# A two-layer decoder step on one core: the S5 tail, the first products and the sine table re-sequenced over four engines

## The chip, the cores and the metric

The kernel runs on one core of a Trainium2 chip. The metric is the device time of one execution in microseconds. Before the change it is 369.06 us (median of 3 runs, 368.89 to 369.34). Five engines run their own instruction streams in order and meet in semaphores: TensorE (PE in the profile, its weight loads PEld), VectorE (DVE), ScalarE (ACT), GpSimd (POOL) and SyncE (SP, which here only issues DMAs).

## The reference

264 tokens (256 of a prompt, 8 single-token samples) pass through two layers. In each, the normalised input goes through one projection, `w_in`, whose 3088 columns feed four head groups; their gated outputs go through `w_out` and are added to the input:

```
h = rmsnorm(x);  proj = h @ w_in
S5:   complex state recurrence over time, y = gelu(C s + D u),  y *= sigmoid(y @ w_glu)
HGRN: gated scan, log_f from hg_f                      -> head rmsnorm
GLA:  gated scan, gate = logsigmoid(lr @ w_up + b)/16  -> head rmsnorm   (lr: 16 columns of proj)
RET:  retention with rotary                            -> head layernorm
x = x + concat(each * silu(z)) @ w_out
```

The new states of all four groups are outputs too. After the second layer comes a last rmsnorm. S5 needs tables of powers of its complex decay, that is exponentials and sines of the parameters, which the kernel computes itself.

## The kernel before

Everything is kept transposed: 128 channels on the partitions, the 264 tokens along the free axis. `w_in` is cut into 25 chunks of 128 columns (`CHUNKS`); the chunk of the GLA low-rank gate, `C_LR`, has 16 real columns and 112 of zeros. SP streams each chunk in two halves of 256 KB through a ring of 12 slots; `project` (L497, by `product`) multiplies a chunk by the 8 tiles of `h` into one of three PSUM banks, and ACT or DVE must have emptied the bank that was used three steps earlier (`ring_free`) before it is written again. A fp32 matmul stands in the trace as two instructions, so a chunk is 16 of them.

The order on each engine is written out by hand at the end of its block: PE's `for i in range(NCH - 1)` runs the chunks in order and hangs the small stages between them (five `level` stages of the gated scans after chunks 7 to 11, then transposes, block states, rotary, retention scores, S5 response and inputs after chunks 18 and 19). After chunk 23 come `s5_outputs` and `gated_outputs` in two parts each, `ret_outputs`, `sample_outputs(0)`, chunk 24, `sample_outputs(1)`, `ret_means`, `glu_gate`, `head_norms`, then the eight products of `w_out`; two of these are fp32, six use operands split in two parts.

DVE starts with `s5_phases` (L1037), which holds a short exponential of the step sizes (the call of `accurate_exp` at its top) and then the phase tables. Then `scale_x` makes `h`, and in layer 0 `accurate_sines` (L1063) and `s5_coefficients` finish the tables; `s5_c` and `s5_b` build the S5 matrices from them (three operations each and part). `gate` makes the gates of the scans from ACT's `gate_logs`, `level_operands` and `level_scores` serve the five levels. `s5_relay` (L1186) copies the S5 input from token order to block order, 24 copies on 32 partitions each; `s5_scan` runs the recurrence; `s5_gelu`, ACT's tanh and `s5_back` (L1381) make the S5 output, the last again with 20 such copies; `gather_outputs` fetches the other groups' outputs, prompt and samples, and the retention state. Then squares, gates, `center`, `s5_mix` and `head_mix` make the operand of `w_out`.

POOL clears three tiles, then multiplies sample states by their decays and issues the DMAs that split the weights of three `w_out` products; ACT negates these weights at L974 between its last silu and the tanh of the gate. SP copies sample values through DRAM to all partitions (`sample_values`, three kinds of four DMAs, one kind behind each of the first `w_out` chunks).

Of the kernel before, what the change touches and what calls it, by code (L numbers as in the profile page):

```python
# [25 lines left out]
ALU = mybir.AluOpType  # L26
# [25 lines left out]
WSLOTS = 6  # L52
EPS = 1e-6
# [5 lines left out]
(C_LR, C_F0, C_F1, C_Q0, C_Q1, C_GQ, C_GK, C_I0, C_I1, C_GV0, C_GV1,  # L59
 C_RQ, C_RK, C_RV0, C_RV1, C_U0, C_U1) = range(NP)  # L60

CHUNKS = [2048, 768, 896, 512, 640, 1536, 1664, 1024, 1152, 1792, 1920, 2320, 2448, 2576, 2704, 0, 128,
# [66 lines left out]
def build(nc, xt, w_in, w_out, par_d, s5m, w_glu, w_up, s5_in, hg_in, gla_in, ret_in, cst, msk,  # L129
          y_out, s5p_out, hgp_out, glap_out, retp_out, s5s_out, hgs_out, glas_out, rets_out):  # L130
    with ExitStack() as ctx:
# [39 lines left out]
        osq = lev[:, KT * TT:(KT + 6) * TT].rearrange("p (g t) -> p g t", g=6)  # L171
# [80 lines left out]
        wup_in, angles_ready = sem("wup_in"), sem("angles_ready")  # L252
# [6 lines left out]
        vs_out, vb_in = sem("vs_out"), sem("vb_in")  # L259
        hi_in = [sem(f"hi_in{i}") for i in range(BY_DMA)]  # L260
# [119 lines left out]
        def _(sp):  # L380
# [25 lines left out]
            for layer in range(DEPTH):  # L406
                for i in range(NCH):
                    chunk(w_in[layer, i])
                    if layer == 0 and i == 1:
                        sp.dma_start(wup[0:16, :, :], w_up).then_inc(wup_in, 16)  # L410
                        sp.dma_start(s5m_t[:, :, :, :], s5m[0]).then_inc(s5m_in, 16)
# [21 lines left out]
                for i in range(KT):  # L433
# [5 lines left out]
                    if i < 3:  # L439
                        sample_values(layer, i)  # L440
# [3 lines left out]
                    if i == 4:  # L444
                        sp.wait_ge(s5f_ready, layer + 1)
                        sp.wait_ge(s3_ready, layer + 1)
                        sp.wait_ge(ss_ready, layer + 1)
                        sp.wait_ge(st_ready, layer + 1)
# [15 lines left out]
        def _(pe):  # L464
# [34 lines left out]

            def low_rank(layer):  # L500
                pe.wait_ge(chunk_evac, layer * NCH + C_LR + 1)
                if layer == 0:
                    pe.wait_ge(wup_in, 16)
                nc.tensor.matmul(wk[:, 1, 0:TT], wup[0:16, layer, :], lr_t[0:16, :], start=True, stop=True)\
# [172 lines left out]
            def sample_outputs(layer, part):  # L677
# [4 lines left out]
                if part == 0:  # L682
                    for t in range(2):
                        for b in range(NS):
                            a = 2 * (NS * t + b)
                            nc.tensor.matmul(wk[0:64, 4, a:a + 2], ss[:, t, b, :], qs_hg[:, t, b, :], start=True, stop=True)  # L686
                else:
                    for n in range(2):
                        for b in range(NS):
                            a = 32 + 4 * (NS * n + b)  # L690
                            mm = nc.tensor.matmul(wk[0:64, 4, a:a + 4], ss[:, 2 + n, b, :], qs_gr[:, n, b, :],  # L691
                                                  start=True, stop=True)
# [20 lines left out]
            def head_norms(layer):  # L713

                for t in range(6):
# [3 lines left out]
                    nc.tensor.matmul(ring_bank(layer, i)[:, 0:TT], c("mean64"), osq[:, t, :], start=True, stop=True)\  # L719
# [24 lines left out]
            pe.wait_ge(zero_ready, 1)  # L744
            for layer in range(DEPTH):
                mean_square(layer)
                for i in range(NCH - 1):
                    project(layer, i)
                    if i == C_F0:
# [50 lines left out]
        def _(act):  # L800
# [118 lines left out]

            def s5_evac(layer, n):  # L920
# [6 lines left out]
            for layer in range(DEPTH):  # L927
# [5 lines left out]
                evac(layer, C_LR, lr_t[0:16, :])  # L933
                evac(layer, C_F0, x3[:, 0, :])
                evac(layer, C_F1, x3[:, 1, :])
# [54 lines left out]
        def _(dve):  # L990
# [45 lines left out]

            def s5_phases():  # L1037

                lr, li = par(Q_LR, LS), par(Q_LI, LS)
                accurate_exp(sw[:, 0, :], par(Q_LS, LS), [sw[:, n, :] for n in (1, 2, 3)])  # L1040
# [20 lines left out]
                s5_turns(sw[:, 2, :], c("mult")[:, 0:NPW], sinp, cosp, None)  # L1061

            def accurate_sines():  # L1063

                x1 = sincos[:, :, :, :].rearrange("p a s m -> p (a s m)")
                x2, q = (z[:, 0:x1.free_size()] for z in (turns, turnr))
                step(ts(x1, x1, 2 * np.pi, None, ALU.mult))
                settle()
                step(tt(x2, x1, x1, ALU.mult))
                settle()  # L1070
                series = [(-1.0) ** (k // 2) / factorial(k) for k in range(19, 1, -2)]
                step(ts(q, x2, series[0], None, ALU.mult))
                for term in series[1:]:
                    settle()
                    step(stt(out=q, in0=q, scalar=term, in1=x2, op0=ALU.add, op1=ALU.mult))
                settle()
                step(stt(out=x1, in0=q, scalar=1.0, in1=x1, op0=ALU.add, op1=ALU.mult))
                settle()
# [106 lines left out]

            def s5_relay(layer):  # L1186

                dve.wait_ge(chunk_evac, layer * NCH + C_U1 + 1)
# [470 lines left out]
```

## Time and profile before

| | |
|---|---|
| time, median of 3 runs | 369.06 us |
| the profiled execution's own time | 366.72 us |
| its span, first to last instruction | 364.9 us |
| PE busy | 337.0 us (92%) |
| DVE busy | 252.1 us (69%) |
| ACT busy | 96.9 us (27%) |
| POOL busy | 33.5 us (9%) |
| mean granted clock of TensorE | 0.986 |

The span is one execution; its own time is 1.8 us longer than the span. In the tables below a start is in us from the span's start, `xN` says how many instructions a row merges, and the brackets say how long the engine sat idle before the row and what ended the wait. PE's rows overlap a little, since its ends are modelled: distances are read from start to start.

### The profile page before, as it was taken

To read this page: it belongs to the slowest core of one execution; us is meant where nothing else is said; L and a number is where in the kernel's file an instruction comes from. 1 tells how busy PE (TensorE), PEld (TensorE's weight loads), DVE (VectorE), ACT (ScalarE), POOL (GpSimd) and SP (SyncE) were. 2 spreads that over 40 slices of the span, in tenths; PEclk is the share of its full clock that TensorE was granted. 3 is DMA by queue.
4 is the path that set the end of the run, shared out by engine and by line. 5 is a ranking of instruction groups with operands and counts; after the bars stand their busy time and mean duration, and the time that the engine had idled before them with its cause. 6 is when DMAs were issued, how large, how long until landed. Compare 5 with 4: busy or idle time off the path is not lost.

```text
span 364.9 us, 6344 instructions
## 1 busy us (share of the span) xinstructions
PE 337.0 (92%) x2532; PEld 287.5 (79%) x2532; DVE 252.1 (69%) x577; ACT 96.9 (27%) x194; POOL 33.5 (9%) x59
## 2 busy tenths in 40 slices
PE   3399999889999999989979999999999999998992
PEld 2278888667889898869967888887888989876991
DVE  2889349964976983994749446893695893887454
ACT  4015200142322011373410720015123001047321
POOL 3007000004100000340000000000500000120000
PEclk9989999999999999999999999999999999989998
DMA  8926753313341500599803473323351430569203
GB/s 277 357 89 188 275 178 91 112 58 114 114 148 64 170 3 4 176 215 369 288 14 118 146 259 113 114 72 104 96 169 59 139 91 2 167 122 280 94 0 119
DMA packets 27917, 50.80 MB, mean 139 GB/s; under 512 B 6240, under 2 KB 6768, under 8 KB 27888
## 3 DMA queue, kind: packets, MB, share of 16 engines
q1 hardware_dynamic: 25872, 44.01, 36.1%
q0 software_dynamic: 1728, 6.29, 7.4%
q8 instruction: 20, 0.33, 0.4%
q10 hardware_dynamic: 288, 0.09, 0.1%
q14 instruction: 9, 0.07, 0.1%
HBM read 46.75 MB, written 3.64 MB: 138 GB/s over the span
## 4 chain that ended last, share of the span: by engine, by line
PE 83%; DVE 11%; ACT 3%; DMA 2%; issue 1%; DVEq 0%; ACTq 0%
PE pr L480 50%; PE pr L740 10%; PE wk L535 2%; PE wk L580 2%; PE wk L657 2%; DMA cs<-in_cst 2%; DVE att L1295 1%; PE wk L649 1%; PE wk L595 1%; PE wk L691 1%; PE wk L584 1%; PE wk L686 1%; DVE h L998 1%; PE wk L548 1%; PE wk L524 1%; PE wk L551 1%
## 5 line engine op out<-in xcount | busy, mean ns | idle before, releaser
L480 PE MATMUL pr<-h,wring 128*128 128x264 f32 x800 | 186.8, 391 | 7.3 <-DVE h L998 7.3
L480 PEld LDWEIGHTS pr<-h,wring 128*128 128x128 f32 x800 | 150.4, 191 | 35.4 <-issue 9.8
L740 PE MATMUL pr<-a_hi,w_hi 128*128 128x264 f32 x96 | 27.6, 288 | 0.0
L740 PE MATMUL pr<-a_lo,w_hi 128*128 128x264 f32 x96 | 27.2, 283 | 0.0
L740 PE MATMUL pr<-a_hi,w_lo 128*128 128x264 f32 x96 | 27.2, 283 | 0.0
L918 ACT ACTIVATE zs<-pr 128x264 f32<-128x264 f32 x16 | 6.2, 390 | 71.6 <-PE pr L480 71.6
L1295 DVE COPY_PREDICATED att<-masks,wk 128x512 f32<-128x512 int32 x20 | 17.6, 951 | 1.0
L835 ACT ACTIVATE h<-x 128x264 f32<-128x264 f32 x24 | 9.5, 420 | 32.9 <-DVE x L1439 30.6
L1439 DVE TENSOR_TENSOR x<-x,pr 128x264 f32<-128x264 f32 x16 | 6.8, 428 | 16.4 <-PE pr L740 12.6
L740 PEld LDWEIGHTS pr<-a_lo,w_hi 128*128 128x128 f32 x96 | 18.1, 188 | 0.1
L740 PEld LDWEIGHTS pr<-a_hi,w_hi 128*128 128x128 f32 x96 | 18.1, 188 | 0.1
L740 PEld LDWEIGHTS pr<-a_hi,w_lo 128*128 128x128 f32 x96 | 18.0, 187 | 0.0
L847 ACT ACTIVATE v<-pr 128x264 f32<-128x264 f32 x12 | 4.7, 388 | 47.3 <-PE pr L480 47.3
L480 PE MATMUL pr<-zs,wring 128*128 128x264 f32 x64 | 15.1, 389 | 0.6 <-DVE zs L1423 0.6
L480 PEld LDWEIGHTS pr<-zs,wring 128*128 128x128 f32 x64 | 12.0, 190 | 3.4 <-DVE zs L1423 1.4
L580 PEld LDWEIGHTS wk<-qe,k 64*128 64x128 f32 x160 | 10.5, 187 | 5.0 <-issue 2.8
L1541 POOL COPY f<-eb 128x24 f32<-128x24 f32 x2 | 0.4, 203 | 147.2 <-DVE kd L1334 147.2
L580 PE MATMUL wk<-qe,k 64*128 64x64 f32 x160 | 12.2, 270 | 1.4 <-DVE qe L1284 1.4
L1562 POOL DMA_DIRECT2D w_hi<-in_w_out x6 | 3.6, 616 | 105.0 <-PE wk L669 105.0
L998 DVE SCALAR_TENSOR_TENSOR h<-x,parm,u 128x264 f32<-128x264 f32 x24 | 10.0, 486 | 4.3 <-ACT u L814 4.3
L1180 DVE COPY tmat<-wk 32x128 f32<-32x128 f32 (+3 forms) x16 | 7.7, 483 | 7.5 <-PE wk L524 7.1
L494 PE MATMUL wk<-h,ones_d 128*128 128x264 f32 x16 | 5.9, 550 | 5.7 <-ACT h L835 5.7
(272 smaller groups left out, 528.4 us busy)
## 6 DMA issues: line engine op xcount, KB each, us to landing
wring<-in_w_in SPq DMA_DIRECT2D x100, 256.0 KB, 2.8
wring<-in_w_out SPq DMA_DIRECT2D x20, 256.0 KB, 6.0
w_hi<-in_w_out POOLq DMA_DIRECT2D x6, 512.0 KB, 4.4
w_lo<-in_w_out POOLq DMA_DIRECT2D x6, 512.0 KB, 8.8
x<-in_xt SPq DMA_DIRECT2D x2, 528.0 KB, 4.9
out_y<-h SPq DMA_DIRECT2D x4, 264.0 KB, 2.1
s5m_t<-in_s5m SPq DMA_DIRECT2D x2, 512.0 KB, 7.1
ss<-in_hg_in SPq DMA_DIRECT2D x2, 512.0 KB, 4.0
```

The costliest lines, as they stand in the source:

```text
L480: mm = nc.tensor.matmul(ring_bank(layer, i)[:, 0:TT], wring[:, slot, n, :], act_in[:, k, :], start=(k == 0), stop=(k == KT - 1))
L494: mm = nc.tensor.matmul(wk[:, 0, 0:TT], ones_d[:, :], h[:, k, :], start=(k == 0), stop=(k == KT - 1))
L535: mm = nc.tensor.matmul(wk[:, 2 * n + s // 4, a:a + NS + SC], gtr[:, n, s, :], ub[:, s, 0:NS + SC], start=True, stop=True)
L580: nc.tensor.matmul(wk[:, 2 * (n % 2) + r, a:a + 64], k3[rows, t, S], right[rows, t, T, :], start=True, stop=True)
L657: mm = nc.tensor.matmul(wk[rows, kind, TP * t + BL * b:TP * t + BL * b + BL], st, q, start=False, stop=(t == 1 and b == NB - 1), skip_grou ...
L740: mm = nc.tensor.matmul(ring_bank(layer, i)[:, 0:TT], w[:, j % WSLOTS, n, :], a[:, k, :], start=(k == 0 and p == 0), stop=(k == KT - 1 and ...
L835: step(fn(h[:, k, :], x[:, k, :], ACT.Square), sq_ready)
L918: step(fn(zs[:, i - NP, :], ring_bank(layer, i)[:, 0:TT], ACT.Silu), chunk_evac)
L998: step(stt(out=h[:, k, :], in0=x[:, k, :], scalar=par(weights + k), in1=rstd, op0=ALU.mult, op1=ALU.mult), signal)
L1180: step(cp(qrt(tmat, q)[:, 4 * half:4 * half + 4, 32 * (3 - q):P], src))
L1295: step(nc.vector.copy_predicated(out[:, :, part], mk, data[:, :, part]), lvl_used if g else None)
L1439: step(tt(x[:, m, :], x[:, m, :], ring_bank(layer, NCH + 8 + m)[:, 0:TT], ALU.add), out_used)
```

## The change

Seven things are edited together.

1. PE multiplies `ones_d` by itself seven times before it waits for the first squares.
2. `s5_phases` moves behind the first `scale_x` and `lower_bounds`; only the exponential of the step sizes (`s5_steps`) stays ahead. `accurate_sines` moves to POOL, where each fused step becomes two operations (21 in all); DVE waits for it between `level_operands(0)` and `s5_coefficients`. `s5_c` and `s5_b` of layer 0 each come one or two levels later.
3. The first two chunks change places. The low-rank chunk is multiplied in four groups of 32 columns, each group with two of the eight tiles of `h`; the four partial sums are added by the next matmul, which contracts over all 128 partitions with `w_up` in four places. `w_up` so takes four DMAs, which wait for a clearing memset on POOL.
4. `s5_relay` and the copies of `s5_back` move from DVE to ACT.
5. S5 and gated outputs come before chunk 23 instead of after it; both sample outputs, chunk 24 and `glu_gate` follow `ret_outputs` in this order, then `ret_means`.
6. `sample_outputs` alternates between the two 64-column halves of the array and the output partitions; DVE gathers it in eight copies instead of six.
7. SP issues the twelve sample copies together behind the first `w_out` chunk; DVE copies the retention state after `low_operand`, and SP waits for it two chunks later.

```diff
-(C_LR, C_F0, C_F1, ...
+(C_F0, C_LR, C_F1, ...
-        osq = lev[:, KT * TT:(KT + 6) * TT].rearrange("p (g t) -> p g t", g=6)
+        osq = [lev[:, a * TT:(a + n) * TT].rearrange("p (g t) -> p g t", g=n) for a, n in ((0, 4), (KT, 2))]
@@ sync
-                        sp.dma_start(wup[0:16, :, :], w_up).then_inc(wup_in, 16)
+                        sp.wait_ge(wup_zero, 1)
+                        for q in range(4):
+                            sp.dma_start(wup[32 * q:32 * q + 16, :, :], w_up).then_inc(wup_in, 16)
...
-                    if i < 3:
-                        sample_values(layer, i)
+                        for kind in range(3):
+                            sample_values(layer, kind)
@@ tensor
+            def project_low_rank(layer):
+                ring_free(pe, layer, C_LR)
+                for half in range(2):
+                    slot = use[0] % RING
+                    pe.wait_ge(w_in_sem[slot], 16 * (use[0] // RING + 1))
+                    use[0] += 1
+                    for n in range(KH):
+                        mm = nc.tensor.matmul(ring_bank(layer, C_LR)[32 * n:32 * n + 32, 0:TT], wring[:, slot, n, 0:32],
+                                              h[:, KH * half + n, :], start=(half == 0), stop=(half == 1))
+                    mm.then_inc(proj_done if half else half_done, 1)
...
-                nc.tensor.matmul(wk[:, 1, 0:TT], wup[0:16, layer, :], lr_t[0:16, :], start=True, stop=True)\
+                nc.tensor.matmul(wk[:, 1, 0:TT], wup[:, layer, :], lr_t, start=True, stop=True)\
...
+                    for b in range(NS):
+                        for t in range(2):
+                            a = 2 * b
+                            nc.tensor.matmul(wk[64 * t:64 * t + 64, 4, a:a + 2], ss[:, t, b, :], qs_hg[:, t, b, :],
+                                             start=True, stop=True)
...
+            for n in range(WARM):
+                nc.tensor.matmul(wk[:, 1, 0:P], ones_d[:, :], ones_d[:, :], start=True, stop=True)
...
-                    if i == C_F0:
+                    if i == C_F1:
                         low_rank(layer)
...
-                s5_outputs(layer, 0)
-                gated_outputs(layer, 0)
-                s5_outputs(layer, 1)
-                gated_outputs(layer, 1)
+                    if i == NCH - 3:
+                        s5_outputs(layer, 0)
+                        gated_outputs(layer, 0)
+                        s5_outputs(layer, 1)
+                        gated_outputs(layer, 1)
                 ret_outputs(layer)
                 sample_outputs(layer, 0)
+                sample_outputs(layer, 1)
                 project(layer, NCH - 1)
-                sample_outputs(layer, 1)
+                glu_gate(layer)
                 ret_means(layer)
-                glu_gate(layer)
                 head_norms(layer)
@@ scalar
+            def s5_relay(layer):          # the 24 copies, as fn(dst, src, ACT.Copy)
+            def s5_back(layer):
+                act.wait_ge(yb_ready, layer + 1)
+                ...                       # 20 copies, as fn(dst, src, ACT.Copy, scale=0.5)
...
                 evac(layer, C_U1, u[:, 1, :])
+                s5_relay(layer)
                 turned(layer, 5, krt[:, :, :])
                 for i in range(NP, NCH):
-                    if i == NCH - 1:
+                    if i == NCH - 2:
                         for n in range(2):
                             s5_evac(layer, n)
+                    if i == NCH - 1:
                         act.wait_ge(tin_ready, layer + 1)
                         step(fn(yt2, yt2, ACT.Tanh, scale=GELU_C), tanh_ready)
+                        s5_back(layer)
                     silu(layer, i)
@@ vector
-            s5_phases()
+            s5_steps()
             for layer in range(DEPTH):
                 scale_x(layer, Q_NORM + layer * KT, h_ready)
                 if layer == 0:
                     lower_bounds()
-                    accurate_sines()
-                    s5_coefficients()
-                    dve.wait_ge(set_ready, 1)
-                s5_c(layer, 0)
+                    s5_phases()
                 if layer:
+                    s5_c(layer, 0)
                     s5_c(layer, 1)
                 gate(layer)
                 dve.wait_ge(k3_ready, layer + 1)
                 level_operands(layer, 0)
+                if layer == 0:
+                    dve.wait_ge(ph_ready, 1)
+                    s5_coefficients()
...
                 for n in range(NL):
                     level_operands(layer, n + 1)
                     level_scores(layer, n)
-                    if n == 1 and layer == 0:
-                        s5_c(layer, 1)
-                    if n in (2, 3):
-                        s5_b(layer, n - 2)
+                    if layer == 0 and n in (1, 2):
+                        if n == 1:
+                            dve.wait_ge(set_ready, 1)
+                        s5_c(layer, n - 1)
+                    if n in (3, 4):
+                        s5_b(layer, n - 3)
...
                 s5_gelu(layer)
-                s5_back(layer)
-                gather_outputs(layer)
+                for kind in range(2):
+                    gather_outputs(layer, kind)
+                s5_gelu_end(layer)
+                gather_outputs(layer, 2)
+                gather_samples(layer)
...
                 low_operand(layer)
+                ret_states(layer)
@@ gpsimd
+            def accurate_sines():
+                pool.wait_ge(turns_ready, 1)
+                ...
+                for term in series[1:]:
+                    settle()
+                    step(ts(q, q, term, None, ALU.add))
+                    settle()
+                    step(tt(q, q, x2, ALU.mult))
+                ...
+                step(tt(x1, q, x1, ALU.mult), ph_ready)
```

## Rows read from the trace of the kernel before

**Rows 1.** The page, part 4: shares of the chain that ended last.

```profile
PE 83%; DVE 11%; ACT 3%; DMA 2%; issue 1%; DVEq 0%; ACTq 0%
```

**Rows 2.** Busy time by stretch: busy us (instructions), granted clock, DMA share, GB/s.

```profile
core 0: us, PE busy (x) PEld busy (x) DVE busy (x) ACT busy (x) POOL busy (x), PEclk, DMA share, GB/s
17.40:26.10 8.70, 8.70 (x32) 6.97 (x32) 7.36 (x28) 1.00 (x4) 0.00 (x0) 0.83 0.27 87
314.40:332.60 18.20, 16.17 (x109) 13.14 (x109) 14.81 (x45) 8.07 (x13) 3.64 (x5) 0.91 0.79 193
```

**Rows 3.** Timeline of the beginning: start, duration, engine, line, operation, shapes.

```profile
5.13 2.77 ACT L835 ACTIVATE h<-x 128x264 f32<-128x264 f32 x8 [2.21 <-DMA x<-in_xt]
5.70 5.95 PE L494 MATMUL wk<-h,ones_d 128*128 128x264 f32 x16 [5.70 <-ACT h L835]
...
9.86 0.18 DVE L1041 TENSOR_TENSOR sw<-parm,sw 128x16 f32<-128x16 f32 x1
...
12.11 0.42 ACT L814 ACTIVATE u<-u 128x264 f32<-128x264 f32 x1
...
16.75 3.32 DVE L998 SCALAR_TENSOR_TENSOR h<-x,parm,u 128x264 f32<-128x264 f32 x8
...
17.39 8.80 PE L480 MATMUL pr<-h,wring 128*128 128x264 f32 x32 [5.74 <-DVE h L998]
```

**Rows 4.** Pieces of the chain: start, us, engine, tile, line, instructions.

```profile
26.82 21.56 PE pr L480 x96
...
89.27 0.42 PE wk L609 x32
...
118.61 14.29 PE pr L480 x64
...
136.11 0.79 PE wk L657 x28
...
146.00 1.96 PE wk L686 x32
147.96 3.76 PE pr L480 x16
...
287.05 14.29 PE pr L480 x64
```

**Rows 5.** Timeline of DVE and PE before and in layer 0's levels.

```profile
42.64 0.69 DVE L1268 TENSOR_TENSOR qe<-q,eb 128x512 f32<-128x512 f32 x1 [4.75 <-ACT eb L891]
...
59.16 1.49 DVE L1149 TENSOR_TENSOR ca_im<-are,s5m_t 128x1280 f32<-128x1280 f32 x1
...
64.96 0.66 PE L580 MATMUL wk<-qe,k 64*128 64x64 f32 x8 [0.68 <-DVE qe L1284]
...
66.42 1.23 DVE L1163 TENSOR_TENSOR lev<-gre,s5m_t 128x1024 f32<-128x1024 f32 x1
```

**Rows 6.** Timeline of POOL's tensor operations in layer 0.

```profile
29.19 1.54 POOL L1526 TENSOR_TENSOR s5t<-s5i,are 128x64 f32<-128x64 f32 x1 [25.20 <-DVE gim L1131]
...
33.73 0.30 POOL L1529 TENSOR_TENSOR s5t<-s5i,are 128x64 f32<-128x64 f32 x1
...
88.74 4.04 POOL L1555 TENSOR_TENSOR ss<-ss,f 128x512 f32<-128x512 f32 x4
```

**Rows 7.** Groups by line: count, busy us, mean ns, idle before.

```profile
L900 ACT ACTIVATE qh<-qe,cs 128x256 f32<-128x256 f32 x16 | 6.6, 495 | 0.0
```

**Rows 8.** Timeline of the tail, layer 0, last row layer 1.

```profile
128.58 0.68 DVE L1237 TENSOR_TENSOR si<-lev 128x504 f32<-128x504 f32 x1
...
152.04 2.94 ACT L974 ACTIVATE w_lo<-w_hi 128x1024 fp32r<-128x1024 f32 x3
...
157.43 0.61 ACT L976 ACTIVATE rqm<-wk 128x528 f32<-128x528 f32 x1 [2.46 <-PE wk L701]
...
159.35 0.95 ACT L981 ACTIVATE qm<-pr 128x264 f32<-128x264 f32 x3
...
162.09 2.35 DVE L1423 TENSOR_TENSOR zs<-zs,qm 128x264 f32<-128x264 f32 x6 [0.28 <-ACT qm L984]
...
332.11 2.34 DVE L1423 TENSOR_TENSOR zs<-zs,qm 128x264 f32<-128x264 f32 x6 [1.48 <-ACT qm L984]
```

More of the change, by code:

```diff
@@ L52 @@
 WSLOTS = 6
+WARM = 7
 EPS = 1e-6
@@ L682, in sample_outputs @@
                 if part == 0:
[L683 to L686, printed above, removed]
-                else:
[L688 to L691, printed above, removed]
+                    for b in range(NS):
[3 more added lines that the diff above has]
+                                             start=True, stop=True)
+                else:
+                    for b in range(NS):
+                        for n in range(2):
+                            a = 2 * NS + 4 * b
+                            mm = nc.tensor.matmul(wk[64 * n:64 * n + 64, 4, a:a + 4], ss[:, 2 + n, b, :], qs_gr[:, n, b, :],
                                                   start=True, stop=True)
@@ L918, in silu @@
                 step(fn(zs[:, i - NP, :], ring_bank(layer, i)[:, 0:TT], ACT.Silu), chunk_evac)
+            def s5_relay(layer):
+                settle()
+                if layer:
+                    act.wait_ge(y_done, layer * 2)
+                for a in range(4):
+                    src = qrt(u, a)[:, :, 0:TP].rearrange("p t (k j) -> p t k j", j=SL)
+                    for q in range(4):
+                        dst = qrt(ub, q)[:, :, NS:NS + SC].rearrange("p (t s) k -> p t s k", t=2)[:, :, a, :]
+                        step(fn(dst, src[:, :, :, 3 - q], ACT.Copy))
+                    for n, dst in enumerate((qrt(ub, 3)[:, :, NS + SC:], qrt(ub, 0)[:, :, 0:NS])):
+                        step(fn(dst.rearrange("p (t s) k -> p t s k", t=2)[:, :, a, :], qrt(u, a)[:, :, TP:TT], ACT.Copy),
+                             u_ready if a == 3 and n == 1 else None)
+            def s5_back(layer):
+                act.wait_ge(yb_ready, layer + 1)
+                yv = yb.rearrange("p (t s k) -> p t s k", t=2, s=4)
+                for a in range(4):
+                    for j in range(4):
+                        dst = qrt(yg, a)[:, :, 0:TP].rearrange("p t (k j) -> p t k j", j=SL)[:, :, :, j]
+                        step(fn(dst, qrt(yv, j)[:, :, a, 0:SC], ACT.Copy, scale=0.5))
+                    step(fn(qrt(yg, a)[:, :, TP:TT], qrt(yv, 0)[:, :, a, SC:], ACT.Copy, scale=0.5),
+                         yg_ready if a == 3 else None)
             def s5_evac(layer, n):
@@ L1060, in s5_phases @@
                 settle()
[L1061 to L1078, printed above, removed]
+                s5_turns(sw[:, 2, :], c("mult")[:, 0:NPW], sinp, cosp, turns_ready)
             def s5_turns(turn, mult, dst_sin, dst_cos, signal):
@@ L1364, in gather_outputs @@
                     step(cp(qrt(retf, hd), qrt(wk, hd)[:, 3, 64 * hd:64 * hd + 64]), st_ready if hd == 3 else None)
-                dve.wait_ge(so_done, layer + 1)
-                for hh in range(2):
-                    rows = slice(64 * hh, 64 * hh + 64)
-                    step(cp(o[rows, 0:2, TP:TT], wk[0:64, 4, 0:32].rearrange("p (t b h) -> p t b h", t=2, h=2)[:, :, :, hh]))
-                    for n in range(2):
-                        src = wk[0:64, 4, 32 + 32 * n:64 + 32 * n].rearrange("p (b t h) -> p t b h", t=2, h=2)[:, :, :, hh]
-                        step(cp(o[rows, 2 + 2 * n:4 + 2 * n, TP:TT], src), o_ready if hh and n else None)
             def s5_gelu(layer):
@@ L1407, in square_outputs @@
                 settle()
-                step(tt(osq[:, part, :], o[:, part, :], o[:, part, :], ALU.mult), osq_ready)
+                step(tt(osq[part.start // 4], o[:, part, :], o[:, part, :], ALU.mult), osq_ready)
             def head_gates(layer, tiles):
```

87 lines of the change are left out of this document (49 added, 38 removed).

## The prediction

> **What bounds the kernel now.** I read the chain that ended last first: 83% of it is PE's, 11% DVE's [rows 1]. So what counts is PE's own work, and the places where PE waits. The timeline then gives four such places. At the beginning PE has its squares at 5.70 us but its first product at 17.39, released by DVE's `h` [rows 3]. In layer 0's levels PE waits 0.68 us for DVE's operands, at 64.96 and about as much at the two levels behind it [rows 5]. In the tail of each layer PE waits for DVE's and ACT's chain up to `head_mix` (162.09 and 332.11) [rows 8]. And the table by stretch shows the granted clock at 0.83 in the first products and 0.91 in layer 1's tail [rows 2]: of the two levels, 1.2 and 2.4 GHz, part of these ran at the lower. A chunk at the higher clock is 21.56 / 6 = 3.59 us, 0.2246 us an instruction [rows 4].
>
> **The change part by part.** All times are of the profiled execution, 366.72 us; the median of the runs, 369.06, stands 2.34 above it, and I carry the sum over as a difference.
>
> *The beginning.* DVE's order made PE wait: rstd was there at 12.11 + 0.42 = 12.53, `scale_x` started at 16.75 because of `s5_phases`, whose moved part runs from 9.86 to 16.75, 6.9 us [rows 3]. Left ahead is the short exponential, done at 9.86. The mean square is slow itself: 16 instructions in 5.95 us, 0.372 each, against 0.2246 later, so it ran mostly at the lower clock. The seven extra matmuls (14 instructions, half as wide) run between `ones_d` and the first square, while PE sat idle for 5.70 us; if they bring the clock up in time, the mean square takes 16 x 0.2246 + 0.2 = 3.8 and ends at 9.5 instead of 11.65 (ACT's squares end at 7.9). rstd takes as long as now (12.53 - 11.65 = 0.9): 10.4. From `scale_x` to PE's first product it is 17.39 - 16.75 = 0.64: PE starts at 11.0. Gain 6.4 us. If the clock stays down until the squares are done, PE starts at 12.53 + 0.04 + 0.64 = 13.2, gain 4.2. I take 6.4; PE is then idle for some 1.5 us instead of 5.7 before the products, so I expect them at the higher clock from the start.
>
> *First products.* Two chunks took 8.80 us [rows 3] for 2 x 3.59: 1.6 of it the clock, which goes. The low-rank chunk keeps 16 instructions, but in four column groups. Rows for small tiles show groups running beside each other: 32 instructions of a 32 x 64 tile in 0.42 us, 13 ns each; 28 on alternating halves (128 x 64) 0.79 us, 28 ns each; 32 on one half alone 1.96 us, 61 ns each [rows 4]. Two groups thus run at twice the pace of one and the small tiles more than twice. No row has four groups with 264 moving columns; the bounds are 3.59 (no overlap) and 3.59 / 4 = 0.9. I take 0.9 + 0.25 for entering and leaving the form, 1.15, since the nearest rows by form all overlap. Gain 2.4 a layer, and 0.15 on `low_rank`, which no longer uses a 16-row tile: 1.6 + 2.6 = 4.2 in layer 0, 2.6 in layer 1. It is on the path in layer 1 too, because the gate's logs start 3 us earlier there as well and DVE's `s5_c` (six operations behind `scale_x`) ends just when they are ready. The chunk swap costs nothing: ACT's copy of the low-rank result hides under the third chunk. Three more DMAs and a wait in SP's queue delay chunks 2 to 5 by about 1 us of issue; PE needs chunk 2 only at 15.8.
>
> *Phases, sines, coefficients.* DVE now does `scale_x` 10.4 to 13.7, lower bounds (about 1.8), `s5_phases` (6.9) to 22.5. PE's second, third chunk and `low_rank` end at 19.9, ACT's logs 3.2 later, 23.1; so `gate` does not wait for the phases, but only just. POOL's 21 operations on 160 columns start at 22.5. The bounds per operation: 0.30 us (64 columns, DVE idle) and 1.54 (64 columns while DVE runs operations of 1.5 us back to back); 512 columns take 1.01 with DVE mostly idle [rows 6]. Between 64 and 512 columns, 160 are 0.45; with a wait each I take 0.5, so 10.5 us, done at 33.0 to 34. DVE comes to the wait at about 32.7 (PE's chunk for `level_operands(0)` ends at 30.7; today DVE idles 4.75 us there [rows 5], and that idle time is POOL's cover). Behind the wait on DVE stand the coefficients (3.1 us) and all later levels; but the next operand is wanted only after level 0, at 38.8, and one level later 1.4 us more are free, so nothing is lost up to 36. Cost taken: 0; if the cover is gone, each us past 36 costs one.
>
> *Levels.* In layer 0 DVE has three S5 parts between the operands of the second and last level, before and after. Before: one `s5_c` (3 x 1.49) and two `s5_b` (3 x 1.23). After: two `s5_c` and one `s5_b` [rows 5]. DVE sets the end there, so 0.8 us is lost. The `s5_b` behind the last level hides under the next chunk (3.59) and `rotate`.
>
> *Relay and block copies on ACT.* ACT's price for 32 x 128 is not in the trace. ACT runs eight 264-column operations in 2.77 us, 0.35 each; 256 columns with a scale per partition stand at 0.495 each [rows 3, 7]. 0.2 is the pace if it goes with the columns; I take 0.25: relay 24 copies, at most 6 us, `s5_back` 20 copies, 5 us. The relay lies behind the last evacuation before two chunks of slack: nothing. `s5_back` runs from the tanh (behind chunk 23) and must be done by the end of chunk 24; it ends 1.4 us ahead of it. At 0.495 a copy it would end some 3.5 us later and cost 2 us a layer. DVE loses 5.5 us twice a layer, none of it on the path.
>
> *Outputs one chunk earlier.* `s5_outputs` then wants the scan at 118.61 + 3/4 x 14.29 = 129.3; DVE has it at 128.58 + 0.68 = 129.26 [rows 4, 8]. No stall, no reserve.
>
> *Tail.* PE's order up to the end of chunk 24 holds the same work, with both sample stages instead of one, each on two halves: at 28 instead of 61 ns, 1.0 instead of 1.96. Chunk 24 ended at 147.96 + 3.76 = 151.7 [rows 4]; now 151.9 (1.96 - 2 x 1.0, and 0.2 for the change of form). Gathering, squares and the first gates, done by DVE after it before, now run beside it. What is late next is ACT: it negates the weights (2.94, from 0.4 after chunk 24) to 155.3, then the gate's tanh, which waited for PE at 157.43 and now for ACT. From the tanh to the first logarithms it is 159.35 - 157.43 = 1.92 (a table load in it): 157.2. From there to `head_mix` 162.09 - 159.35 = 2.74: 160.0. Gain 2.1 in layer 0. In layer 1 the same point lies 287.05 - 118.61 = 168.44 later, 328.4; before it was 332.11: gain 3.7, the 1.6 more being the lower clock [rows 2, 8], which came after sample outputs with idle time behind them; that place is now a chunk.
>
> *Hidden.* SP's twelve sample copies together put two `w_out` chunks behind them by about 2 us, wanted 35 us later. The retention state adds 1 us to DVE under the first product of `w_out`, and SP's wait for it moves along.
>
> Sum: -6.4 - 4.2 + 0.8 - 2.1 - 2.6 - 3.7 = -18.2. Profiled 348.5, median **350.9 us**.
>
> *A rule against it.* POOL's first operations of 64 columns took 1.54 us while DVE ran, 0.30 as DVE stopped [rows 6]. The Trainium skill, "GPSIMD Engine Reference", section "Key points", says that GpSimd shares its memory interfaces with VectorE and contends with two-input instructions there; the rows agree (1.54 against 0.30). Weighed by that alone the sines would be held during the whole gate; that is the last rival below.
>
> **The rivals.**
> - *The warm-up does not reach the mean square.* For it: at 17.39 PE went on at the lower clock though it had worked until 11.65. Against: then it had idled 5.7 us, now 1.5. Price 2.2: 353.1.
> - *ACT's copies are slow*, 0.495 each; they are small, which speaks against. 2 us a layer: 354.9.
> - *The column groups do not overlap* with 264 columns. Against it are all three small-tile rows. Price 2.4 a layer: 355.7. With this and the first the change would do less than it says.
> - *The sines end late in part*, at 40: 4 us, 354.9.
> - *Slower: POOL is held by DVE throughout.* 21 x (1.54 + 0.1) = 34.4 from 22.5: 56.9, past 36 by 20.9, all of it on DVE's path through the levels: 371.8. It takes more than 1.5 us for each operation to decide. Against it: DVE itself idles before `level_operands(0)` and again in its wait, so the holding ends by itself.
>
> **How the numbers follow.** Forecast 0.53 (own range 348.5 to 353), warm-up 0.17, ACT 0.11, groups 0.07, sines in part 0.07, sines throughout 0.04, other losses that leave no gain 0.01. The range takes in the middle rivals and, below, levels without loss and a better tail: 347.5 to 357.5. A difference under 0.2% (0.7 us) can't be told from none. Faster 0.95, same 0.01, slower 0.04.
>
> **What would show it.** PE's first product at 11.0, with instructions at 0.22 us from the start; the low-rank chunk in about 1.2 us; `s5_coefficients` at 33 to 34 and no wait of DVE on POOL over 2 us; 0.5 us for POOL's operations; the sample stages in 1 us each; `head_mix` 41.4 us after the end of `s5_inputs` in both layers (43.5 and 45.1 before). Wrong would be a PE wait on `qe` in the levels of more than some 1 us each, on `yg` before `glu_gate`, or on the scan before `s5_outputs`.

## The result, and the profile after

The changed kernel takes 357.63 us (median of 4 executions, 356.61 to 357.86) against 369.20 for the kernel before in the same job (368.89 to 369.43): ratio 0.9696 [0.9655, 0.9736], 11.6 us less. It is faster, as forecast, but the forecast was 350.9 with a range that ended at 357.5, 0.13 us below the median. The two profiled executions stand 8.99 us apart (366.72 and 357.73). The kernel before was profiled in one of its quicker executions (over all jobs they spread from 365.06 to 370.05), the changed kernel in a middling one, so the 2.34 us that I carried over as the distance to the median was for the second kernel nothing.

The path splits into stretches at points that both traces have: PE's first product (L486), the first level (L598, `wk<-qe,k`), the transposes behind the levels (L613, `wk<-cs,k`), the last start of `s5_inputs` (L553), DVE's `head_mix` (L1444). Each number is the distance between two start times of the timeline; the forecast is the row of before less the term that the prediction gave.

| stretch, us | before | after | forecast |
|---|---|---|---|
| start to first product | 17.39 | 12.94 | 11.0 |
| to the first level, layer 0 | 30.92 | 26.76 | 26.7 |
| first level to transposes, layer 0 | 29.58 | 32.21 | 30.4 |
| last `s5_inputs` to `head_mix`, layer 0 | 43.75 | 43.52 | 41.6 |
| first product to first level, layer 1 | 29.48 | 28.45 | 26.9 |
| last `s5_inputs` to `head_mix`, layer 1 | 45.34 | 43.55 | 41.6 |
| all others together | 168.46 | 168.46 | 168.5 |

Five of the six stretches miss 1.6 to 1.9 us each, 9.1 in sum. So no single step failed: four did, one of them in both layers.

The chain that ended last (the page, part 4, to be held against [rows 1]): PE's share fell by 15 points; ACT's rose by 7, POOL's by 4, DVE's by 2.

```profile
PE 68%; DVE 13%; ACT 10%; POOL 4%; issue 2%; DMA 1%; DVEq 0%; POOLq 0%; ACTq 0%
```

The beginning, from the timeline (start, duration, engine, line; it answers to [rows 3]):

```profile
1.04 3.35 PE L765 MATMUL wk<-ones_d 128*128 128x128 f32 x14 [1.04 <-DVE ones_d L1467]
...
5.36 5.94 PE L500 MATMUL wk<-h,ones_d 128*128 128x264 f32 x16 [0.96 <-ACT h L860]
...
11.76 0.42 ACT L839 ACTIVATE u<-u 128x264 f32<-128x264 f32 x1
12.30 3.32 DVE L1051 SCALAR_TENSOR_TENSOR h<-x,parm,u 128x264 f32<-128x264 f32 x8 [2.59 <-ACT u L839]
12.94 3.80 PE L486 MATMUL pr<-h,wring 128*128 128x264 f32 x16 [1.64 <-DVE h L1051]
...
16.67 1.10 PE L514 MATMUL pr<-h,wring 128*32 128x264 f32 x16
```

The reordering of DVE did what it should: `scale_x` follows rstd at once (12.18 and 12.30), and the first product 0.64 later. But the mean square took 5.94 us, as long as before (5.95); PE had stood idle for 0.96 us between the warm-up and the squares. The low-rank chunk in four column groups took 1.10 us for 16 instructions; the next chunk started 1.03 us after it.

POOL's sines and those who wait for them, layer 0 (timeline of POOL, DVE and PE; to [rows 5, 6]):

```profile
24.52 0.62 POOL L1548 TENSOR_SCALAR sincos<-sincos 128x160 f32<-128x160 f32 x1 [20.28 <-DVE sincos L1131]
...
26.31 1.25 POOL L1553 TENSOR_SCALAR lev<-lev 128x160 f32<-128x160 f32 x1
27.65 0.82 POOL L1556 TENSOR_SCALAR lev<-lev 128x160 f32<-128x160 f32 x1
...
37.46 0.61 POOL L1556 TENSOR_SCALAR lev<-lev 128x160 f32<-128x160 f32 x1
38.15 0.52 POOL L1558 TENSOR_TENSOR lev<-lev 128x160 f32<-128x160 f32 x1
...
39.46 0.52 POOL L1562 TENSOR_TENSOR sincos<-lev,sincos 128x160 f32<-128x160 f32 x1
```

```profile
40.01 0.24 DVE L1141 TENSOR_TENSOR are<-mag,sincos 128x80 f32<-128x80 f32 x1 [4.32 <-POOL sincos L1562]
```

```profile
45.86 0.33 PE L598 MATMUL wk<-qe,k 64*128 64x64 f32 x2 [0.79 <-DVE qe L1308]
```

```profile
58.18 0.66 PE L598 MATMUL wk<-qe,k 64*128 64x64 f32 x8 [1.65 <-DVE qe L1308]
...
65.45 0.66 PE L598 MATMUL wk<-qe,k 64*128 64x64 f32 x8 [1.51 <-DVE qe L1308]
```

POOL was done at 39.98, not at 33 to 34, and DVE waited 4.32 us. PE waited 0.79 us for DVE's operands at the second level, 1.65 at the fourth and 1.51 at the fifth; e1 below shows which part of this is due to POOL.

The tail of layer 0 (timeline of DVE, PE and ACT; to [rows 4, 8]):

```profile
122.59 0.68 DVE L1261 TENSOR_TENSOR si<-lev 128x504 f32<-128x504 f32 x1
...
155.88 1.46 DVE L1444 TENSOR_TENSOR zs<-zs,qm 128x264 f32<-128x264 f32 x4 [0.80 <-ACT qm L1037]
```

```profile
123.33 0.44 PE L566 MATMUL wk<-ub,tmat 128*128 128x72 f32 x2
...
140.51 1.10 PE L704 MATMUL wk<-qs_hg,ss 128*64 128x2 f32 x32
141.47 1.08 PE L710 MATMUL wk<-qs_gr,ss 128*64 128x4 f32 x32
142.48 5.51 PE L486 MATMUL pr<-h,wring 128*128 128x264 f32 x16
148.14 2.05 PE L720 MATMUL wk<-u,s5m_t 128*128 128x264 f32 x8
```

```profile
139.89 1.80 ACT L966 ACTIVATE u<-lev 32x128 f32<-32x128 f32 x4 [0.82 <-DVE lev L1413]
...
147.87 0.21 ACT L967 ACTIVATE u<-lev 32x16 f32<-32x16 f32 x1
148.11 0.39 ACT L943 ACTIVATE zs<-pr 128x264 f32<-128x264 f32 x1
148.40 2.94 ACT L1027 ACTIVATE w_lo<-w_hi 128x1024 fp32r<-128x1024 f32 x3
151.24 0.60 ACT L1029 ACTIVATE rqm<-wk 128x528 f32<-128x528 f32 x1
```

Four copies of 32 x 128 take 1.80 us, 0.45 each; all twenty run from 139.89 to 148.08, and the glu matmuls (`glu_gate`, L720) start at 148.14. The same moment is the end of chunk 24, which took 5.51 us instead of 3.8: two causes on one place. And the granted clock (stretches; busy us and count of each engine, PEclk, DMA share, GB/s; to [rows 2]):

```profile
core 0: us, PE busy (x) PEld busy (x) DVE busy (x) ACT busy (x) POOL busy (x), PEclk, DMA share, GB/s
12.94:21.80 8.86, 8.86 (x50) 6.87 (x51) 7.38 (x33) 1.64 (x6) 0.00 (x0) 1.00 1.01 365
142.48:148.00 5.52, 5.51 (x20) 4.13 (x16) 3.96 (x13) 5.20 (x14) 0.00 (x0) 0.69 0.64 229
305.30:323.10 17.80, 16.46 (x128) 12.74 (x128) 9.19 (x24) 16.18 (x34) 4.33 (x6) 0.90 0.53 135
183.76:187.20 3.44, 3.44 (x9) 2.65 (x9) 3.31 (x8) 0.00 (x0) 0.00 (x0) 0.50 0.00 0
```

The first products ran at the higher level (1.00). In chunk 24 of both layers, and at the beginning of layer 1, the clock fell to the lower one (0.50 from 183.76 to 187.20). A stretch that holds both levels shows a value between them (0.69 in chunk 24 of layer 0).

### The profile page after: what moved, and what is told of

The parts are those of the page before. It is cut to its first block, busy times and chain, and to the rows that moved or that the text cites. A ratio compares the mean times of both kernels' runs of the same rounds, so it can differ in the third digit from the quotient of the medians.

```text
span 355.9 us, 6388 instructions
## 1 busy us (share of the span) xinstructions
PE 333.9 (94%) x2546; PEld 282.8 (79%) x2546; DVE 229.8 (65%) x481; ACT 128.3 (36%) x282; POOL 43.9 (12%) x81
## 4 chain that ended last, share of the span: by engine, by line
PE 68%; DVE 13%; ACT 10%; POOL 4%; issue 2%; DMA 1%; DVEq 0%; POOLq 0%; ACTq 0%
PE pr L486 39%; PE pr L759 10%; ACT u L966 4%; DVE att L1319 2%; PE wk L553 2%; DVE h L1051 2%; PE wk L675 2%; PE wk L500 2%; ACT w_lo L1027 2%; POOL lev L1556 2%; PE wk L598 1%; POOL lev L1558 1%; PE wk L566 1%; PE wk L667 1%; PE wk L613 1%
## 5 line engine op out<-in xcount | busy, mean ns | idle before, releaser
L486 PE MATMUL pr<-h,wring 128*128 128x264 f32 x768 | 184.2, 397 | 3.2 <-DVE h L1051 3.2
L486 PEld LDWEIGHTS pr<-h,wring 128*128 128x128 f32 x768 | 146.6, 194 | 31.5 <-issue 5.9
L598 PEld LDWEIGHTS wk<-qe,k 64*128 64x128 f32 x160 | 10.5, 187 | 7.6 <-DVE qe L1308 5.2
L598 PE MATMUL wk<-qe,k 64*128 64x64 f32 x160 | 12.2, 270 | 3.9 <-DVE qe L1308 3.9
L486 PE MATMUL pr<-zs,wring 128*128 128x264 f32 x64 | 15.1, 389 | 0.6 <-DVE zs L1444 0.6
L486 PEld LDWEIGHTS pr<-zs,wring 128*128 128x128 f32 x64 | 12.0, 190 | 3.4 <-DVE zs L1444 1.4
L966 ACT ACTIVATE u<-lev 32x128 f32<-32x128 f32 x32 | 13.8, 430 | 2.4 <-DVE lev L1413 1.6
```

Source lines behind the costliest of these rows:

```text
L486: mm = nc.tensor.matmul(ring_bank(layer, i)[:, 0:TT], wring[:, slot, n, :], act_in[:, k, :], start=(k == 0), stop=(k == KT - 1))
L598: nc.tensor.matmul(wk[:, 2 * (n % 2) + r, a:a + 64], k3[rows, t, S], right[rows, t, T, :], start=True, stop=True)
L966: step(fn(dst, qrt(yv, j)[:, :, a, 0:SC], ACT.Copy, scale=0.5))
```

## The experiments

Each was timed in five rounds beside the kernel before, whose medians were 368.45 (a1, e1 to e3), 368.75 (f1 to f4), 369.65 (g1, g2) and 369.36 us (h1, h2). The stretches of their profiles, measured as above, the tail cut in two at the start of the glu matmuls (L720 in the changed kernel):

| run | start | to level 0 | levels, layer 0 | to glu 0 | glu to mix 0 | to level 0, layer 1 | to glu 1 | glu to mix 1 | median us | ratio to before |
|---|---|---|---|---|---|---|---|---|---|---|
| a1 | 13.43 | 26.76 | 32.22 | 35.78 | 7.74 | 28.45 | 35.81 | 7.74 | 358.15 | 0.9709 [0.9656, 0.9761] |
| e1 | 12.55 | 26.77 | 30.42 | 35.80 | 7.74 | 26.76 | 35.81 | 7.74 | 354.33 | 0.9618 [0.9569, 0.9668] |
| e2 | 12.73 | 26.76 | 33.05 | 33.80 | 8.69 | 28.45 | 35.49 | 7.97 | 355.93 | 0.9681 [0.9637, 0.9726] |
| e3 | 12.83 | 26.76 | 33.03 | 34.16 | 9.98 | 26.76 | 34.23 | 8.86 | 356.39 | 0.9682 [0.9635, 0.9729] |
| f1 | 11.10 | 26.76 | 32.22 | 35.81 | 7.74 | 26.76 | 35.81 | 7.74 | 354.70 | 0.9624 [0.9595, 0.9654] |
| f2 | 12.52 | 26.76 | 33.06 | 35.81 | 7.75 | 26.76 | 35.81 | 7.74 | 357.88 | 0.9713 [0.9681, 0.9746] |
| f3 | 12.67 | 26.76 | 33.06 | 33.81 | 7.23 | 26.76 | 33.81 | 6.64 | 351.81 | 0.9559 [0.9518, 0.9601] |
| f4 | 11.44 | 26.76 | 30.43 | 33.80 | 7.08 | 28.33 | 33.80 | 8.48 | 348.91 | 0.9468 [0.9435, 0.9501] |
| g1 | 10.85 | 29.48 | 31.23 | 35.81 | 7.74 | 29.48 | 35.81 | 7.74 | 359.36 | 0.9743 [0.9701, 0.9786] |
| g2 | 13.15 | 26.77 | 32.23 | 35.81 | 7.74 | 28.45 | 35.80 | 7.74 | 356.55 | 0.9666 [0.9627, 0.9705] |
| h1 | 12.50 | 26.76 | 33.06 | 35.82 | 7.75 | 26.76 | 35.82 | 7.74 | 356.57 | 0.9649 [0.9600, 0.9698] |
| h2 | 11.65 | 26.76 | 30.42 | 33.80 | 7.34 | 26.76 | 33.80 | 7.24 | 348.85 | 0.9463 [0.9422, 0.9503] |

**a1: the changed kernel again,** nothing edited.

> The changed kernel as it is, as the base for the three kernels that run beside it. Every theory: 357.6 us within 1.2, ratio to before 0.970; in the profile DVE's wait on POOL before the coefficients 4.3 us, the block copies on ACT 8 us.

In this profile the clock did not fall in the tail of layer 0, and the tail was still 35.78 + 7.74. Chunk 24 was early and PE waited (timeline of PE):

```profile
148.63 0.71 PE L720 MATMUL wk<-u,s5m_t 128*128 128x264 f32 x2 [1.82 <-ACT u L967]
```

So the copies set this place by themselves; where the clock falls too, the longer chunk only fills the time beside them.

**e1: the sines on DVE again,** behind the gate.

```diff
                 gate(layer)
+                if layer == 0:
+                    accurate_sines()
...
-                    dve.wait_ge(ph_ready, 1)
+                    dve.wait_ge(set_ready, 1)
                     s5_coefficients()
```

> One part of the change undone: the sines are on DVE again (11 fused operations, 4.1 us), put behind the gate of layer 0, where DVE idles 4.5 us; POOL does none. Theory (the sines on POOL end at 40.0 and make DVE late for all levels): coefficients start at 35.8 instead of 40.0, the transpose behind the last level comes 30.4 us after level 0 instead of 32.2, 1.8 us less in all than the base. Rival (DVE's own S5 parts between the levels set the pace, the wait on POOL is hidden by them): the wait goes, the transpose stays at 32.2, difference within 0.4 us.

The levels took 30.42. DVE needs 4.1 us for the whole series (12 instructions, 28.65 to 32.76), all of it in the gap before `level_operands(0)`, and starts the coefficients at 35.05 instead of 40.01 (timeline of DVE):

```profile
28.65 0.24 DVE L1122 TENSOR_SCALAR sincos<-sincos 128x160 f32<-128x160 f32 x1
28.93 0.33 DVE L1124 TENSOR_TENSOR lev<-sincos 128x160 f32<-128x160 f32 x1
...
29.57 2.84 DVE L1130 SCALAR_TENSOR_TENSOR lev<-lev 128x160 f32<-128x160 f32 x8
32.44 0.32 DVE L1132 SCALAR_TENSOR_TENSOR sincos<-lev,sincos 128x160 f32<-128x160 f32 x1
...
35.05 0.23 DVE L1158 TENSOR_TENSOR are<-mag,sincos 128x80 f32<-128x80 f32 x1
```

PE's waits were 0.71 and 1.50 us at the fourth and fifth level and none at the second (timeline of PE, e1):

```profile
56.00 0.66 PE L598 MATMUL wk<-qe,k 64*128 64x64 f32 x8 [0.71 <-DVE qe L1325]
...
63.27 0.66 PE L598 MATMUL wk<-qe,k 64*128 64x64 f32 x8 [1.50 <-DVE qe L1325]
```

So POOL's sines cost 0.79 us at the second level and 0.94 at the fourth; the wait at the fifth is DVE's own S5 work and stays. Against the sines on DVE behind the gate, the move to POOL cost 1.8 us. The rest of the 4.3 us between the two profiles (a1 and e1) is the beginning of layer 1, where the clock stayed up (1.69), and an earlier start (0.88), which the edit does not touch.

**e2: the twenty copies on DVE again; e3: the same, and the first sample stage ahead of chunk 23.**

```diff
-                        s5_back(layer)                  # ACT, behind the tanh
+                        # DVE, behind s5_gelu_end: 20 x ts(yg, yv, 0.5)
... e3 besides:
                         gated_outputs(layer, 1)
+                        sample_outputs(layer, 0)
                 ret_outputs(layer)
-                sample_outputs(layer, 0)
```

> One part undone: the 20 block copies of the S5 output are on DVE again, behind the same point of its order; everything else as changed. Theory A (ACT's copies at 0.455 us set the tail): they end at about 145.5 instead of 148.1, the gate product starts at 146.4, 1.8 us less in each layer, 3.6 less in all than the base. Theory B (two limits lie side by side: the last chunk runs at the lower clock, 5.5 instead of 3.8 us, and ends at 148.0 whatever the copies do): the gate product starts at 147.9, difference 0 to 0.5 us wherever the clock falls as in the profile.

> As the copies on DVE, and the first sample stage moved ahead of chunk 23, so that two short stages are no longer behind one another before the last chunk. Theory B: the clock stays up, the last chunk takes 3.8 us, the gate product starts at 146.4 and 3.4 us are gained over the base, more than with the copies alone. Theory A: the same as with the copies on DVE alone. If the clock falls for another reason, the last chunk still takes 5.5 us and nothing is gained over the base.

In e2's layer 0 the clock stayed up and the glu matmuls started 2.0 us earlier (33.80); in layer 1 it fell into chunk 24 and 0.3 was left (35.49). But 0.95 came back behind it: DVE gathers and squares only after the copies, and PE waits for it (timeline of PE, e2):

```profile
149.41 0.61 PE L738 MATMUL pr<-lev,cs 128*128 128x264 f32 x2
151.48 2.54 PE L738 MATMUL pr<-lev,cs 128*128 128x264 f32 x10 [1.47 <-DVE v L1421]
```

The gain in time, 2.2 us by the medians, lies between the two theories (3.6, and 0 to 0.5).

In e3 chunk 24 ran at the higher clock in both layers; it did so in layer 0 of a1 and e2 too, so whether the order of the sample stages moves the fall stays open. The stretch behind the glu was no shorter: 8.86 in layer 1. The 9.98 of layer 0 holds the lower clock besides (0.50 from 152.71 to 156.12): the ten instructions that took 2.54 us in e2 took 4.18 there (timeline of PE, e3):

```profile
152.63 4.18 PE L738 MATMUL pr<-lev,cs 128*128 128x264 f32 x10 [1.67 <-DVE v L1421]
```

So with all twenty copies on DVE, PE waits for DVE behind the glu in both orders (1.47 and 1.67 us in layer 0).

**f1 and f2: ten warm-up matmuls instead of seven, and none.**

```diff
-WARM = 7
+WARM = 10        # f2: WARM = 0
```

> Ten warm-up matmuls instead of seven, so that PE works without a gap from 1.04 us to the first square (14 instructions took 3.35 us, 20 take 4.8: to 5.8; the first square is there at 5.36). Theory A, the gap of about 1 us between the warm-up and the mean square was what kept the clock down: the clock rises before 8 us instead of 9 to 10.6, the mean square takes about 4 us instead of 5.6 to 6.4, and PE's first product starts at 11.0 to 11.5 instead of 12.6 to 13.4. The time falls by 1.8 us, to 0.995 of the changed kernel's. Theory B, the warm-up's small matmuls count for nothing: start at 12.6 to 13.9, time unchanged or 0.4 us longer.

> No warm-up matmuls. Theory A, with a gap behind them the seven brought nothing: the clock rises 4 to 5 us after the start of the mean square as before, the mean square takes 5.6 to 6.4 us, PE's first product starts at 12.6 to 13.4, the time stays within 0.3% of the changed kernel's. Theory B, they did bring a part: the mean square takes over 6.5 us and the start comes after 13.8, 1 us or more later.

With ten, PE had no gap ahead of the squares, the granted clock rose at 5.74 us, and the mean square took 3.89 (timeline of PE, f1):

```profile
1.04 4.64 PE L765 MATMUL wk<-ones_d 128*128 128x128 f32 x20 [1.04 <-DVE ones_d L1467]
5.57 3.89 PE L500 MATMUL wk<-h,ones_d 128*128 128x264 f32 x16
11.10 3.80 PE L486 MATMUL pr<-h,wring 128*128 128x264 f32 x16 [1.64 <-DVE h L1051]
```

Without any, the clock rose at 8.81, the mean square took 5.48, and PE started at 12.52 (f2):

```profile
5.40 5.48 PE L500 MATMUL wk<-h,ones_d 128*128 128x264 f32 x16 [5.40 <-ACT h L860]
```

With seven, eight of the nine profiles (all but g1's) show the rise at 8.72 to 10.63 us and PE's start at 12.50 to 13.43: there the seven brought nothing. In g1's profile, with the same seven, the clock rose at 4.80 and PE started at 10.85. With ten, the three profiles (f1, f4, h2) show the rise at 5.74 to 7.07 and the start at 11.10 to 11.65. Ten are longer (4.64 us against 3.35) and leave no gap; which of the two counts no run separates. Of the 4.0 us between the profiles of f1 and a1, 2.3 are the start; 1.7 are the beginning of layer 1, where f1's clock stayed up.

The Trainium skill, "TensorE: Matmul & The Clock Gate", Part 1, says that what the chip watches runs freely, so that the same kernel warms up after different counts from run to run; the rises at 4.80 (g1), 9.68 (the changed kernel) and 10.63 us (a1) of the same beginning agree.

**f3: the copies divided, ten on each engine, and ACT's negations ahead of its last silu.**

```diff
-                for a in range(4):            # ACT
+                for a in range(2, 4):         # ACT; a = 0, 1 on DVE
...
-        (three negations behind silu(24))
+        (three negations behind s5_back, ahead of silu(24))
```

> The twenty block copies of the S5 part are divided, ten on DVE (0.27 to 0.30 us each) and ten on ACT (0.455 each), and ACT negates the weights ahead of its last silu. Theory A, the tail waits for the copies only because one engine makes all twenty, and behind them for ACT's negations: both halves are done about 4.6 us after the tanh, ahead of the end of chunk 24; from the last s5_inputs to the glu matmuls 33.8 us (35.8 in the changed kernel), from there to head_mix about 6.7 (7.74), the time 5.5 to 6 us under the changed kernel's, and 2 less for each layer in which the lower clock falls into chunk 24. Rival, DVE becomes the bound behind the glu matmuls, as with all twenty copies on it: 33.8 and 8.0 to 8.7, a gain of 1 to 3.5 us in both layers together.

33.81 in both layers, and 7.23 and 6.64 behind it: by these stretches 2.5 and 3.1 us less than a1, 5.6 in all, as the first theory had it (the medians stand 6.3 apart). How much of it comes from the divided copies and how much from the earlier negations is not separated. In layer 0 DVE reaches `head_mix` without a wait, so there it has become the bound (timeline of DVE, f3):

```profile
140.45 1.19 DVE L1417 TENSOR_SCALAR u<-lev 32x128 f32<-32x128 f32 x4
...
152.77 1.04 DVE L1447 SCALAR_TENSOR_TENSOR zs<-v,parm,zs 128x264 f32<-128x264 f32 x2
153.92 2.35 DVE L1455 TENSOR_TENSOR zs<-zs,qm 128x264 f32<-128x264 f32 x6
```

**f4: all of it together.**

> Everything together: sines back on DVE behind the gate, ten warm-up matmuls, copies divided, negations ahead. If the places are independent of each other the gains add up: 1.8 from the sines, 1.8 from the start, 5.5 to 6 from the tails, 9.3 in sum, about 348.8 us where the changed kernel has 358.1 (0.974 of it, 0.947 of the kernel before). If DVE is the bound that all of them share, the tails gain 1 to 3.5 only and the time is 351 to 353.5.

348.91 us: by the medians the gains add up (9.2 us below a1, 9.3 expected). The profiled execution was the slowest of its six (350.44); its stretches give 7.8, because in layer 1 the tail gained only 1.3. There a negation waited 2.63 us for its weights (timeline of ACT), and silu and the glu tanh stood behind it, hence the 8.48:

```profile
309.90 1.06 ACT L1022 ACTIVATE w_lo<-w_hi 128x1024 fp32r<-128x1024 f32 x1 [2.63 <-DMA w_hi<-in_w_out]
```

**g1: the low-rank chunk as a plain product; g2: the relay on DVE.**

```diff
-                    if i == C_LR:
-                        project_low_rank(layer)
-                    else:
-                        project(layer, i)
+                    project(layer, i)
... g2: the 24 copies of s5_relay in DVE's block, behind s5_chunk_angles
```

> The low-rank chunk is again a plain product of 128 columns, everything else as changed. Theory A, the four column groups take 2.6 us off the path (1.03 us instead of 3.6): from PE's first product to the first level 29.3 us (26.76 in the changed kernel) in layer 0 and 29.3 in layer 1 where the clock stays up; in layer 0 the stretch behind it, which DVE's wait for POOL's sines sets, gives most of that back (32.2 down to 30.4), so the time rises by about 3.4 us to 361.5. Rival, DVE's scaling and the gate's work behind it set both stretches whatever the chunk costs: 27 to 28 us, and the time within 1 us of the changed kernel's.

> The 24 copies of the relay are DVE's again, behind the chunk angles, everything else as changed. Theory A, the relay lies beside other work on either engine: DVE idles 4.96 us in the changed kernel before it copies tmat, the copies take 5.6, and what is left over comes close to nothing or makes the last s5_outputs wait for the scan by some 0.6 us (it is there 0.1 us ahead now): from the transposes to s5_inputs 40.4 as before, the tail 35.8 to 36.4, the time 0 to 1.2 us longer. Rival, the move of the relay brought 2 us or more a layer, because the earlier s5_outputs rest on it: 362 us or more.

g1: 29.48 in both layers, 2.72 more than the 26.76 with column groups. The levels gave about 1 back, since DVE's wait for POOL shrank to 0.66 us, although the clock fell once in them (at 66.2; it did so at 66.8 to 67.4 in e2, e3, f2, f3 and h1 too, whose levels took 33.0 instead of 32.2). The time rose by 1.2 us over a1 instead of 3.4. The profile shows where the rest went: the start was 2.6 us earlier and the clock stayed up at the beginning of layer 1, where a1's fell. g2: every stretch behind the start is as in a1; the relay is hidden on either engine.

**h1 and h2: six idle-time matmuls behind the mean square of layer 1,** in the changed kernel and in f4.

```diff
                 mean_square(layer)
+                if layer:
+                    for n in range(6):
+                        nc.tensor.matmul(wk[:, 1, 0:P], ones_d[:, :], ones_d[:, :], start=True, stop=True)
```

> Six idle-time matmuls (12 instructions, some 1.4 us) behind the mean square of layer 1, where PE waits 1.55 us for DVE's scaling; everything else as changed. Five profiles of the changed kernel and its variants show the clock at 0.50 for 3.4 us from the beginning of layer 1 (first stretch 28.4 us), six do not (26.76). Theory A, PE's gap there is what lets the clock fall: it stays at 1.00 from 175 to 190 us, the stretch is 26.76, and the time falls by the share of executions that lost 1.7 us, 0.5 to 1.7 us. Rival, the clock falls for what PE did earlier, or at a time of its own: falls between 177 and 188 us stay possible, and the time is within 0.5 us of the changed kernel's.

> The same six matmuls in the version with everything together (sines on DVE, ten warm-up matmuls, copies divided, negations ahead), whose profile showed the clock falling at 177.4 us. Theory A: no fall there, layer 1's first stretch 26.76 instead of 28.33, 0.5 to 1.7 us under that version's 348.9. Rival: within 0.5 us of it.

Both profiles show 26.76 there and no fall (h1, stretch around the boundary):

```profile
180.40:190.40 10.00, 9.25 (x59) 6.96 (x58) 7.40 (x12) 2.02 (x5) 0.00 (x0) 1.00 0.25 63
```

Yet six of the eleven profiles of the changed kernel and its variants without the six matmuls show no fall either, and the times (0.9649 beside 0.9709, 0.9463 beside 0.9468) overlap. That PE's gap is what lets the clock fall there is not shown; that the fall costs 1.7 us is (28.45 against 26.76).

No run undoes the new place of `s5_phases`, the earlier S5 and gated outputs, the two halves of `sample_outputs` or the order of SP's copies; what these brought is read from the stretches of the changed kernel alone.

## Why the prediction was wrong

What held, by its own steps. DVE's new order at the beginning: the part of the 6.4 us that needs no clock, 4.2, came (4.45). The first products: -4.16 against -4.2, and g1 gives the column groups and `low_rank` 2.72 us where I took 2.55. The scan in time for the earlier `s5_outputs`: done at 123.27, wanted at 123.33. The levels' 0.8: 0.84 where POOL does not hold DVE up (e1, 30.42 against 29.58). The first products at the higher clock (1.00). The sample stages: 1.0 us each by their starts (140.51, 141.47, 142.48). The relay at nothing (g2). From the glu's tanh to `head_mix` 4.64 us, against 1.92 + 2.74. What moved to the end of the list, the outputs and the states, cost nothing. Of the signs that the prediction named, three came: DVE's wait on POOL (4.32), PE's on `qe` of more than 1 us (1.65), and its wait before `glu_gate` (1.82 in a1).

What failed, four sizes:

- "I take 6.4": the rival *the warm-up does not reach the mean square* came true, at 1.9 us (a start of 12.94 instead of 11.0) against its 2.2; f1 with ten had 1.84 of it back. The warm-up was over after 3.35 us, 0.96 before the first square; I had set neither its end nor this gap against the row of the first square.
- "with a wait each I take 0.5, so 10.5 us": POOL took 15.5 us, from 24.52 to 39.98. With DVE idle its operations take 0.61 and 0.52 us and follow each other every 0.65 on average, 13.7 for 21; that is 3.2 of the 7 us by which it ended later than the 33 of the forecast. 1.8 are the longer operations beside DVE's work (up to 1.25), 2.0 the later start, which the beginning passed on. Rival *the sines end late in part*: 1.8 us on the path (e1) against its 4. The later start moved the limit of 36 too, by 1.9, so that about 2.0 of the 4 us remained (an estimate from 39.98, 36 and the two starts). The rows of 64 and 512 columns, from which I read 0.45, were products of two tensors; these took 0.52 here, an operation of a tensor and a scalar 0.61 on the same columns, and some 0.08 us lies between one and the next. The Trainium skill, "GPSIMD Engine Reference", section "Key points", has elementwise work about twice as fast on DVE; by that, DVE's 0.24 and 0.33 in e1 would give an estimate of 0.48 and 0.66. POOL's rows agree in the sum (0.61 + 0.52) but not one by one.
- "I take 0.25": ACT's copies cost 0.45. The rival *ACT's copies are slow* was set aside because they are small; its price (0.495, 2 us a layer) was right: the tails missed by 1.9 in each layer, and with the copies on DVE the glu matmuls of layer 0 started 2.0 earlier (e2 against a1).
- In layer 1 I gave the first stretch only its column groups. The clock fell there in this profile and took 1.7 of the 2.6 back. That a kernel whose clock falls at other places than before can lose by it stood in no rival.

Two of the three rivals that came were priced well, the sines at twice what they cost. The step that failed beside the four sizes is the one that made a chance of each: they do not exclude each other, and three came together. Each alone led to 353 to 355, their sum (2.2 + 4 + 4 on 350.9) past the end of my range. That the median came out at 357.63 and not 9.1 above the forecast is luck: the 2.34 us of distance to the median, which I added, the changed kernel does not have.

## What to carry to other kernels

Rivals that concern different places add up; the range has to hold two or three of them at once, not the worst one. A block of small strided copies is priced by its count: on ACT 32 x 128 cost 0.45 us, no less than the 0.39 of 128 x 264. Here it paid to divide it between the two engines that wait for each other anyway (f3, 5.6 us, the earlier negations included). Warm-up work is to be laid so that it reaches the first real instruction: with 3.35 us and a gap of about 1 us it brought nothing in eight of nine profiles, with 4.64 us and no gap it helped in all three.

## What the runs showed of the hardware

ACT took 0.43 to 0.45 us for a strided copy of 32 x 128 and 0.39 for 128 x 264 in one piece; DVE took 0.30 for the former (f3). Four column groups with 264 moving columns ran 16 instructions in 1.10 us, where 16 of the plain form stand at 3.80 in the same view. The clock fell at different places in two profiles of the same kernel: in chunk 24 of layer 0 (142.80) in the changed kernel's first profile and not in the second (a1). There PE had not been idle: ahead of it lay the sample stages, 64 instructions of 2 and 4 columns. The same stages lay there in a1, whose clock stayed up, so they alone do not explain the fall; its cause stays open.
